# A two-layer encoder: both mixers written as one stream of half weight blocks with attention rounds between them

## The chip, the cores and the metric

One Trainium2 chip (trn2), one core of it. The time is the device time of one execution in microseconds (us); the figure for a kernel is the median of several runs. Engines are called PE (TensorE; PEld its weight loads), DVE (VectorE), ACT (ScalarE), POOL (GpSimd) and SP (SyncE, here a DMA queue).

## What is computed

Input x is 256 tokens of 1024 float32 channels. Two layers follow, each a token mixer and a channel mixer, each closed by x <- LayerNorm(alpha * x + sublayer(x)).

```python
def hybrid_mixer(x, w_in, w_out, beta_mix, ...):
    proj = x @ w_in                      # 1024 -> 3072: q, k, v of 16 heads of 64
    ...
    oa = diff_attention(...)             # A: 4 heads, two softmax maps each, p0 - lam * p1, RMS norm
    ob = dilated_attention(...)          # B: 6 heads, three dilated windows merged
    oc = neighbourhood_attention(...)    # C: 6 heads, 2-D windows with a position bias
    merged = concatenate([oa, ob, oc])
    return (merged * beta_mix) @ w_out   # 1024 -> 1024
```

The channel mixer of layer 0 is a dense SwiGLU (width 2816), that of layer 1 a SwiGLU with 8 experts of width 3584, two per token. Partial rotary is applied to q and k of A and B.

## The kernel before

All matrix products of weights are made in split form: a value is the sum of a rounded part (`_hi`) and the remainder (`_lo`), and each product takes three matmuls (hi*hi, lo*hi, hi*lo; `with_hi` L1358, `three` L1363). Weights come in units of 1 MB (`UNIT`): SP loads a unit into one of six `raw` buffers (`load` L434), ACT makes `w_hi` (`split_hi` L596), DVE `w_lo` (`split_lo` L857), in three buffers each. So each unit costs ACT and DVE one instruction, and PE 24 matmuls of 512 columns. `w_in` has 12 units (u = 0 to 11: six blocks of 512 columns, each in two halves of the input channels), `w_out` four (two rows of 128 each). The tokens are two tiles (tt = 0, 1). Here a *half block* is one unit for one token tile: 12 matmuls.

Nothing schedules at run time: each engine has its program, written out in order, and waits on semaphores. What stands behind a waiting instruction waits too.

Attention is cut into 20 groups (`GROUPS`, L397): 0 to 3 and 4 to 7 are the A heads for the first and second token tile (one head, two maps), 8 to 10 and 11 to 13 are B (two heads), 14 to 16 and 17 to 19 C (two heads). A round of a group a is, in order: `scores` (L1523, PE, 6 matmuls of 256 columns), `row_max` (L914, DVE; for B and C an addition of a bias first), `exps` (L623, ACT), for A also `mix_maps` (L935, DVE), `prob_transposes` (L1542, PE), `prob_copy` (L638, ACT), `weigh_values` (L1556, PE), and after the last group of a segment `merge` (L947, DVE). `qk_group` (PE L1509, ACT L615, DVE L875) transposes q and k of proj in eight groups of four 128x128 tiles and splits them.

Order before, in each layer (PE L1574 on, ACT L691 on, DVE L1060 on): the input is transposed (`operand`, L1377), then `column_units` (L1391) runs each unit for both token tiles. q/k groups 0 and 1 come after unit 3, scores 0 and 1 after unit 4, and from unit 5 on (`SLOTS`, L415) one A round stands behind each unit. After unit 11 all other q/k groups are made, then rounds 8 to 19 run with nothing between them; three splits for the output projection stand among them (`SPLIT_AFTER`, L417). Then the merged heads are transposed into `xT` (`operand`), and `row_units` (L1424) makes the output projection: units 0 and 1 for each token tile, then 2 and 3. `norm_and_operand` (L1012) follows on DVE.

POOL prepares the position bias of C: `padded_rows` (L520) reads the bias rows with one DMA and writes them to a scratch in HBM; `toeplitz` (L537) reads them back shifted, 2304 pieces of 256 bytes for each of two DMAs, and adds the mask with a tensor_tensor on POOL (L549). In layer 0 SP issues no load from unit 3 on until the scratch is written:

```python
if l == 0 and u == NH:
    sp.wait_ge(scratch_in, 32)
load(BASE_IN[l] + u, columns(w_in[l], u // 2, u % 2, 2, CW))
```

## Time and profile before

| | |
|---|---|
| median of 3 runs | 1332.92 us (1327.78 to 1335.93) |
| profiled execution, its own time | 1329.73 us |
| its span, first to last instruction | 1327.7 us |
| mean granted TensorE clock, of full | 0.945 |
| PE / DVE / ACT / POOL busy | 1250.4 / 904.4 / 707.4 / 58.3 us |
| DMA moved | 300.13 MB, mean 226 GB/s |

Busy time is the sum of an engine's instructions; DMA issues, waits and branches don't count. A row of the order in time gives start, duration, engine, source line, operation, tiles, shapes, how many like it in a row (x8), and in brackets how long the engine had been idle and what ended that. A duration can overlap the next start a little; spacing of starts is the surer measure. The clock is the one granted to TensorE, 1.00 for 2.4 GHz and 0.50 for 1.2 GHz.

### The profile page before, as it was taken

The page shows a single profiled execution, that of the slowest core. Times are in us where ns is not written, and L with a number is a line of the kernel's source. Part 1 is how long each engine was busy: PE and PEld are TensorE (multiplying, and loading weights), DVE is VectorE, ACT ScalarE, POOL GpSimd, SP SyncE. Part 2 cuts the span into 40 slices and gives each one's busy share as a digit, 9 for nine tenths or more (in the row PEclk, how much of TensorE's full clock was granted, in tenths as well). Part 3 has the DMA queues.
Part 4 walks back from the last instruction along what each step waited for, and adds up shares of the span by engine and source line. Part 5 has one row for each costly group of instructions (what it writes and reads, how often), then busy time and mean ns, then how long its engine had stood idle before and what let it go on. Part 6 is the DMA issues. An engine that isn't in the chain of part 4 may idle for free.

```text
span 1327.7 us, 14942 instructions
## 1 busy us (share of the span) xinstructions
PE 1250.4 (94%) x5856; PEld 1028.4 (77%) x5856; DVE 904.4 (68%) x840; ACT 707.4 (53%) x721; POOL 58.3 (4%) x47
## 2 busy tenths in 40 slices
PE   7897999999998999499999999999999999999994
PEld 6676878887876788488888888878888888777883
DVE  3657465444466664568888767878877798886673
ACT  4445344433344452166776655766765576775550
POOL 2200020000042000000000000000000000000000
PEclk9896799999998958599999999999999999999997
DMA  9921165554565000198889888898888889888750
GB/s 294 321 96 64 42 211 192 164 210 165 190 179 193 1 1 0 69 356 305 306 296 317 287 320 280 302 331 312 291 291 317 309 288 323 298 309 289 299 192 35
DMA packets 126788, 300.13 MB, mean 226 GB/s; under 512 B 4938, under 2 KB 7128, under 8 KB 126704
## 3 DMA queue, kind: packets, MB, share of 16 engines
q1 hardware_dynamic: 124304, 291.52, 63.3%
q0 software_dynamic: 2112, 6.87, 1.8%
q8 instruction: 51, 0.84, 0.3%
q10 hardware_dynamic: 288, 0.63, 0.1%
q14 instruction: 33, 0.27, 0.1%
HBM read 297.88 MB, written 1.12 MB: 225 GB/s over the span
## 4 chain that ended last, share of the span: by engine, by line
PE 82%; DVE 6%; issue 4%; ACT 3%; DMA 2%; POOL 2%; DVEq 0%; POOLq 0%; SPq 0%; ACTq 0%
PE bank L1360 19%; PE bank L1361 19%; PE bank L1418 13%; PE bank L1705 12%; PE bank L1446 6%; PE bank L1718 6%; ACT w_hi L601 2%; DMA raw<-in_w_in 1%; PE bank L1669 1%; DVE soft L932 1%; PE bank L1566 1%; PE bank L1685 1%; DVE w_lo L860 1%; DVE neg_max L933 1%; POOL w_lo L558 1%
## 5 line engine op out<-in xcount | busy, mean ns | idle before, releaser
L860 DVE TENSOR_TENSOR w_lo<-raw,w_hi 128x2048 fp32r<-128x2048 f32 x273 | 620.9, 2290 | 319.1 <-ACT w_hi L601 317.7
L601 ACT ACTIVATE w_hi<-raw 128x2048 fp32r<-128x2048 f32 x275 | 523.9, 1917 | 322.8 <-PE bank L1418 161.6
L1360 PE MATMUL bank<-w_hi,xT_hi 128*128 128x512 f32 (+1 forms) x896 | 353.0, 395 | 8.0 <-DVE xT_lo L872 3.2
L1361 PE MATMUL bank<-w_hi,xT_lo 128*128 128x512 f32 (+1 forms) x896 | 348.5, 390 | 0.0
L1418 PE MATMUL bank<-w_lo,xT_hi 128*128 128x512 f32 (+1 forms) x832 | 219.7, 387 | 0.0
L1360 PEld LDWEIGHTS bank<-w_hi,xT_hi 128*128 128x128 f32 x896 | 171.0, 191 | 44.1 <-ACT xT_hi L612 6.1
L1361 PEld LDWEIGHTS bank<-w_hi,xT_lo 128*128 128x128 f32 x896 | 171.0, 191 | 34.2
L1418 PEld LDWEIGHTS bank<-w_lo,xT_hi 128*128 128x128 f32 x832 | 154.6, 189 | 33.0 <-DVE w_lo L860 1.0
L1360 PE MATMUL bank<-w_hi,hT_hi 128*128 128x512 f32 x312 | 123.7, 397 | 1.8 <-issue 1.8
L1361 PE MATMUL bank<-w_hi,hT_lo 128*128 128x512 f32 x312 | 123.0, 394 | 0.0
L1705 PE MATMUL bank<-w_hi,xs 128*128 128x512 f32 x336 | 94.3, 402 | 0.0
L1705 PE MATMUL bank<-w_lo,xs 128*128 128x512 f32 x336 | 91.9, 395 | 0.0
L1446 PE MATMUL bank<-w_lo,hT_hi 128*128 128x512 f32 x312 | 85.1, 394 | 0.0
L1705 PEld LDWEIGHTS bank<-w_lo,xs 128*128 128x128 f32 x336 | 63.3, 188 | 14.7
L1705 PEld LDWEIGHTS bank<-w_hi,xs 128*128 128x128 f32 x336 | 61.3, 189 | 13.2
L1360 PEld LDWEIGHTS bank<-w_hi,hT_hi 128*128 128x128 f32 x312 | 58.8, 188 | 16.0 <-issue 2.4
L1446 PEld LDWEIGHTS bank<-w_lo,hT_hi 128*128 128x128 f32 x312 | 58.8, 188 | 13.8
L1361 PEld LDWEIGHTS bank<-w_hi,hT_lo 128*128 128x128 f32 x312 | 58.8, 188 | 13.4
L562 POOL TENSOR_TENSOR rstd<-var_eps,tab 128x1 f32<-128x1 f32 x8 | 12.2, 1521 | 1090.5 <-DVE var_eps L997 1090.4
L1566 PE MATMUL bank<-proj,soft 128*128 128x64 f32 x256 | 50.7, 362 | 0.0
L1566 PEld LDWEIGHTS bank<-proj,soft 128*128 128x128 f32 x256 | 50.6, 289 | 0.0
L1718 PE MATMUL bank<-w_hi,hs 128*128 128x512 f32 x168 | 47.2, 402 | 0.0
(208 smaller groups left out, 1004.5 us busy)
## 6 DMA issues: line engine op xcount, KB each, us to landing
raw<-in_moe_w_gate SPq DMA_DIRECT2D x70, 1024.0 KB, 5.4
raw<-in_moe_w_up SPq DMA_DIRECT2D x70, 1024.0 KB, 5.5
raw<-in_moe_w_down SPq DMA_DIRECT2D x70, 1024.0 KB, 5.4
raw<-in_w_in SPq DMA_DIRECT2D x24, 1024.0 KB, 8.5
raw<-in_ffn_w_gate SPq DMA_DIRECT2D x11, 1024.0 KB, 5.1
raw<-in_ffn_w_up SPq DMA_DIRECT2D x11, 1024.0 KB, 5.2
raw<-in_ffn_w_down SPq DMA_DIRECT2D x11, 1024.0 KB, 5.0
raw<-in_w_out SPq DMA_DIRECT2D x8, 1024.0 KB, 5.0
```

Of the source, the lines that this page charges most:

```text
L558: nc.gpsimd.tensor_tensor(w_lo[:, split % NH, :], raw[:, split % NR, :], w_hi[:, split % NH, :].bitcast(F32), ALU.subtract).then_inc(lo_do ...
L601: nc.scalar.activation(w_hi[:, n % NH, :], raw[:, n % NR, :], ACT.Copy).then_inc(hi_done, 1)
L860: nc.vector.tensor_tensor(w_lo[:, n % NH, :], raw[:, n % NR, :], w_hi[:, n % NH, :].bitcast(F32), ALU.subtract).then_inc(lo_done, 1)
L932: link(nc.vector.scalar_tensor_tensor(sc, s2, HD ** -0.5, bias, ALU.mult, ALU.add))
L933: nc.vector.tensor_reduce(nm, sc, AX.X, ALU.max, negate=True).then_inc(max_done, 1)
L1360: nc.tensor.matmul(o, hi, wh, start=start, stop=False)
L1361: nc.tensor.matmul(o, lo, wh, start=False, stop=False)
L1418: ins = nc.tensor.matmul(o, xh[:, kt, t], wl[:, k, :], start=False, stop=kt == KT - 1)
L1446: ins = nc.tensor.matmul(bank[:, b0 + 2 * tt + ch, :], xh[:, 2 * i + k, t], wl[:, 2 * k + ch, :], start=False, stop=i == last and k == 1)
L1566: ins = nc.tensor.matmul(bank[:, O_BANK[seg], col:col + HD], probT[:, ga % 2, i * NT + kt, :], proj[:, kt, v0 + h * HD:v0 + (h + 1) * HD], ...
L1705: ins = nc.tensor.matmul(bank[:, b, :], xs[:, kt, :], wv[:, k, :], start=kt == 0 and ready is None, stop=kt == KT - 1 and ready is not None)
L1718: ins = nc.tensor.matmul(bank[:, b0 + ch, :], hs[:, 2 * i + k, :], wv[:, 2 * k + ch, :], start=i == 0 and k == 0 and ready is None, stop=i ...
```

## The change

What it does, in each layer:

- PE goes through the 12 units of `w_in` by half blocks (`column_half`), unit by unit, token tile by token tile. Behind a half block (u, tt) stands what the tables say: `QK_AT` q/k groups, `SLOT_AT` one attention round, `MERGED_AT` transposes of merged heads. 14 of the 20 rounds (A and B) stand in the projection.
- Rounds 14 to 19 (C) stand between the eight half blocks of the output projection, in an order written out (`out_half`). The merged heads are transposed and split in five groups (`merged_group`) into `qk_hi`, `qk_lo`, which are twice as large.
- A round's scores use one PSUM bank instead of two, with the values of an earlier group between the two halves and a wait of PE for its own first half (`score_half`).
- `proj_copy` copies each token tile of proj when it is done. In ACT's and DVE's programs the order follows PE's; splits of the output projection's units 0, 1 and 2 stand in the projection.
- The first rotary moves from after unit 2 to before the split of unit 3 on DVE, the second from u = 6 to (5, 1).
- POOL reads the bias rows in reverse by seven DMAs; the shifted copy goes straight into `bias_c`, and the mask is added by DVE (`masked_bias`) behind (9, 1) instead of by POOL. POOL issues its later DMAs without that wait.
- A's `merge` is cut in `squares` and `merge_a`, one slot apart.

The arithmetic is the same. The diff, cut to its core (of the removed lines only some; they stand in the listing above):

```diff
-            qk_hi = sb("qk_hi", [P, KT, SEQ], F32R, scope=s)
-            qk_lo = sb("qk_lo", [P, KT, SEQ], F32R, scope=s)
+            qk_hi = sb("qk_hi", [P, 2 * KT, SEQ], F32R, scope=s)
+            qk_lo = sb("qk_lo", [P, 2 * KT, SEQ], F32R, scope=s)
             bias_c = sb("bias_c", [P, HC, 6, GRID_W], scope=s)
             soft = sb("soft", [P, 12 * SEQ], scope=s)
...
+        SLOT_AT = {(4, 1): 0, (5, 0): 1, (5, 1): 2, (6, 0): 3, (6, 1): 4, (7, 0): 5, (7, 1): 6, (8, 0): 7, (8, 1): 8,
+                   (9, 0): 9, (9, 1): 10, (10, 0): 11, (11, 0): 12, (11, 1): 13}
+        IN_SLOTS = len(SLOT_AT)
+        FIRST_AT = ((3, 1), (4, 0))
+        QK_AT = {(2, 1): (0, 1), (6, 0): (2, 3), (7, 0): (4,), (10, 0): (5, 6)}
+        QK_BANK = [2, 3, 4, 5, 4, 4, 5, 6]
+        MERGED_AT = {(11, 0): (0, 1)}
+        MERGED_BANK = [4, 5, 7, 0, 1]
+        N_MERGED = len(MERGED_BANK)
+        SCORES_IN = IN_SLOTS + 2
...
-                pool.dma_start(rpb_rows[:], na_rpb[l].rearrange("h r c -> r h c")[
-                    NA_ROWS - ROWS:NA_ROWS + ROWS - 1]).then_inc(pad_in, 16)
+                for r in range(7):
+                    pool.dma_start(rpb_rows[r:r + 1], na_rpb[l].rearrange("h r c -> r h c")[
+                        NA_ROWS + ROWS - 2 - r:NA_ROWS + ROWS - 1 - r]).then_inc(pad_in, 16)
                 nc.gpsimd.memset(bias_c[0:7], 0.0).then_inc(pad_zero, 1)
-                pool.wait_ge(pad_in, 16 * (l + 1))
+                pool.wait_ge(pad_in, 7 * 16 * (l + 1))
...
-                    pool.dma_start(shifted[rl * GRID_W:(rl + 1) * GRID_W], src).then_inc(toeplitz_in, 16)
-                pool.wait_ge(toeplitz_in, 32 * (l + 1))
-                pool.wait_ge(consts_in, 16)
-                mask = const("mask_c").unsqueeze(1).broadcast_to([P, HC * 6, GRID_W])
-                nc.gpsimd.tensor_tensor(bias_c[:].rearrange("p h j c -> p (h j) c"), shifted[:, :, ::-1], mask,
-                                        ALU.add).then_inc(bias_ready, 1)
+                    dst = bias_c[rl * GRID_W:(rl + 1) * GRID_W].rearrange("p h j c -> p (h j) c")
+                    pool.dma_start(dst, src).then_inc(toeplitz_in, 16)
...
+                    for tt in range(NT):
+                        if (u, tt) == (3, 0):
+                            act.wait_ge(lam_summed, l + 1)
+                            nc.scalar.activation(lam_exp[:], lam_sum[:], ACT.Exp).then_inc(lam_exped, 1)
+                        if u % 2:
+                            proj_copy(l, u, tt)
+                        for k in QK_AT.get((u, tt), ()):
                             qk_group(l, k)
-                    if u < U_IN - NH:
...
+                        for m in MERGED_AT.get((u, tt), ()):
+                            merged_group(l, m)
+                        if (u, tt) in FIRST_AT:
+                            exps(l, FIRST_AT.index((u, tt)))
+                        if (u, tt) in SLOT_AT:
+                            a = SLOT_AT[u, tt]
+                            prob_copy(l, a)
+                            if a + 2 < SCORES_IN:
+                                exps(l, a + 2)
+                        if (u, tt) == (1, 1):
+                            static_split(BASE_IN[l] + NH)
+                        if u > 0 and tt == 1:
+                            static_split(BASE_IN[l] + u + NH)
+                qk_group(l, 7)
+                prob_copy(l, 14)
+                exps(l, 16)
+                prob_copy(l, 15)
+                merged_group(l, 2)
+                exps(l, 17)
+                prob_copy(l, 16)
+                static_split(BASE_OUT[l] + NH)
+                exps(l, 18)
+                prob_copy(l, 17)
+                exps(l, 19)
+                merged_group(l, 3)
+                prob_copy(l, 18)
+                static_split(BASE_OUT[l] + 1 + NH)
+                prob_copy(l, 19)
+                merged_group(l, 4)
+                static_split(BASE_OUT[l] + 2 + NH)
+                next_operand(2 * l + 1, BASE_OUT[l] + U_OUT - 1)
                 if l == 0:
...
+            def masked_bias(l):
+
+                dve.wait_ge(toeplitz_in, 32 * (l + 1))
+                v = bias_c[:].rearrange("p h j c -> p (h j) c")
+                mask = const("mask_c")[:, ::-1].unsqueeze(1).broadcast_to([P, HC * 6, GRID_W])
+                nc.vector.tensor_tensor(v, v, mask, ALU.add).then_inc(bias_ready, 1)
...
+                    for tt in range(NT):
+                        if (u, tt) == (1, 1):
+                            if l == 0:
+                                dve.wait_ge(consts_in, 16)
+                            rotary(QA, DIFF, DIFF // 8, 2 * WA // DIFF, "a", rope_a[0], rope_a[1], (l * IN_CHUNKS + 1) * NT)
+                            static_split(BASE_IN[l] + NH)
+                        if (u, tt) == (5, 1):
+                            rotary(QB, HD, HD // 8, 2 * HB, "b", rope_b[:, :, 0], rope_b[:, :, 1], (l * IN_CHUNKS + 3) * NT)
+                        for k in QK_AT.get((u, tt), ()):
                             qk_group(l, k)
...
+                        for m in MERGED_AT.get((u, tt), ()):
+                            merged_group(l, m)
+                        if (u, tt) == (3, 0):
+                            lambda_value(l)
+                        if (u, tt) in FIRST_AT:
+                            a = FIRST_AT.index((u, tt))
+                            row_max(l, a)
+                            mix_maps(l, a)
+                        if (u, tt) in SLOT_AT:
+                            a = SLOT_AT[u, tt]
+                            if a in SEG_END[0:2]:
+                                squares(l, SEG_END.index(a))
+                            if a == SEG_END[2]:
+                                merge(l, 2)
+                            if a + 2 < SCORES_IN:
+                                row_max(l, a + 2)
+                            if a + 2 < SEG_END[1]:
+                                mix_maps(l, a + 2)
+                            if a - 1 in SEG_END[0:2]:
+                                merge_a(l, SEG_END.index(a - 1))
+                        if u > 0 and tt == 1:
+                            static_split(BASE_IN[l] + u + NH)
+                        if (u, tt) == (2, 1):
+                            dve.wait_ge(small_in, 48 + 16 * l)
+                            if l == 0:
+                                split_router()
+                            lambda_terms(l)
+                        if (u, tt) == (9, 1):
+                            masked_bias(l)
+                qk_group(l, 7)
+                merge(l, 3)
+                row_max(l, 16)
+                merged_group(l, 2)
+                row_max(l, 17)
+                static_split(BASE_OUT[l] + NH)
+                row_max(l, 18)
+                merge(l, 4)
+                row_max(l, 19)
+                merged_group(l, 3)
+                static_split(BASE_OUT[l] + 1 + NH)
+                merge(l, 5)
+                merged_group(l, 4)
+                norm_and_operand(2 * l, 4, BASE_OUT[l] + U_OUT - 1, 2 * l + 1)
...
+                    q, k = (q0 + h // 2, slice(qt * P, (qt + 1) * P)), k0 + h // 2
+                    if i:
+                        if between:
+                            between()
+                        pe.wait_ge(score_half, ga + 1)
+                    ins = three(bank[:, ga % 2, i * SEQ:(i + 1) * SEQ], qk_hi[part, q[0], q[1]], qk_lo[part, q[0], q[1]],
+                                qk_hi[part, k, :], qk_lo[part, k, :], True, True)
+                    ins.then_inc(score_psum if i else score_half, 1)
...
+                tile_ready, next_tile, after = operand(
+                    2 * l, token_tile,
+                    lambda tt: pe.wait_ge(ln_done, 2 * NT * l + tt + 1 - NT) if l else pe.wait_ge(x_in[tt], 16), 1 if l else 0)
+                for tt in range(NT):
+                    for part in range(2):
...
+                            if j == 4:
+                                pe.wait_ge(qk_lo_in, 8 * l + 5)
+                        column_half(BASE_IN[l] + u, u % 2, tt, proj_banks(j))
+                        for k in QK_AT.get((u, tt), ()):
...
+                        for m in MERGED_AT.get((u, tt), ()):
+                            merged_group(l, m)
+                        if (u, tt) in FIRST_AT:
+                            qk_ready(l, 2)
+                            scores(l, FIRST_AT.index((u, tt)))
+                        if (u, tt) in SLOT_AT:
+                            a = SLOT_AT[u, tt]
+                            if a + 2 in (SEG_END[1], SEG_END[1] + 2, SEG_END[3]):
+                                qk_ready(l, {SEG_END[1]: 4, SEG_END[1] + 2: 5, SEG_END[3]: 7}[a + 2])
+                            if a - 1 in (0, SEG_END[1]):
+                                pe.wait_ge(proj_in, (l * IN_CHUNKS + {0: 2, SEG_END[1]: 4}[a - 1]) * NT)
+                            scores(l, a + 2, (lambda: weigh_values(l, a - 1)) if a else None)
+                            prob_transposes(l, a)
+
+                pe.wait_ge(m_lo, N_MERGED * l + 2)
+                out_half(l, 0, 0)
+                qk_group(l, 7)
+                weigh_values(l, 13)
+                prob_transposes(l, 14)
+                out_half(l, 1, 0)
...
+                scores(l, 16, lambda: weigh_values(l, 14))
+                prob_transposes(l, 15)
+                merged_group(l, 2)
+                pe.wait_ge(m_lo, N_MERGED * l + 3)
+                out_half(l, 0, 1)
+                scores(l, 17, lambda: weigh_values(l, 15))
+                prob_transposes(l, 16)
+                out_half(l, 1, 1)
+                scores(l, 18, lambda: weigh_values(l, 16))
+                prob_transposes(l, 17)
+                scores(l, 19, lambda: weigh_values(l, 17))
+                merged_group(l, 3)
+                prob_transposes(l, 18)
+                pe.wait_ge(m_lo, N_MERGED * l + 4)
+                out_half(l, 2, 0)
+                weigh_values(l, 18)
+                prob_transposes(l, 19)
+                out_half(l, 3, 0)
+                weigh_values(l, 19)
+                merged_group(l, 4)
+                pe.wait_ge(m_lo, N_MERGED * l + 5)
+                out_half(l, 2, 1)
+                out_half(l, 3, 1)
+                making = operand(2 * l + 1, token_tile, lambda tt: pe.wait_ge(ln_done, 2 * NT * l + tt + 1), 1)
```

## Rows read from the trace of the kernel before

**Rows 1.** The page, part 1: busy time and share of the span.

```profile
PE 1250.4 (94%) x5856; PEld 1028.4 (77%) x5856; DVE 904.4 (68%) x840; ACT 707.4 (53%) x721; POOL 58.3 (4%) x47
```

**Rows 2.** Stretches: start:end, their length, then busy time of each engine, clock, DMA.

```profile
394.60:455.20 60.60, 54.71 (x275) 43.37 (x274) 39.29 (x65) 25.79 (x55) 8.42 (x5) 0.94 0.37 119
455.20:509.00 53.80, 48.85 (x268) 44.44 (x267) 34.41 (x53) 30.30 (x75) 1.12 (x1) 0.59 0.00 1
```

**Rows 3.** PE in order of time, layer 1: start, duration, operation, idle before it.

```profile
384.26 1.07 PE L1418 MATMUL bank<-w_lo,xT_hi 128*128 128x512 f32 x4
...
386.98 1.07 PE L1418 MATMUL bank<-w_lo,xT_hi 128*128 128x512 f32 x4
...
411.75 0.59 PE L1365 MATMUL bank<-qk_hi 32*128 32x256 f32 x2 [5.24 <-ACT soft L632]
...
530.14 1.07 PE L1446 MATMUL bank<-w_lo,xT_hi 128*128 128x512 f32 x4
```

**Rows 4.** PE in order of time, layer 0.

```profile
38.46 1.97 PE L1516 MATMUL bank<-tab,proj 128*128 128x128 f32 x8 [3.88 <-DVE proj L892]
40.08 0.77 PE L1360 MATMUL bank<-w_hi,xT_hi 128*128 128x512 f32 x1
...
44.88 0.40 PE L1360 MATMUL bank<-w_hi,xT_hi 128*128 128x512 f32 x1
...
109.83 0.40 PE L1365 MATMUL bank<-xT_hi,qk_hi 64*128 64x256 f32 x2
...
110.89 1.00 PE L1566 MATMUL bank<-proj,soft 128*128 128x64 f32 x8
...
171.53 0.84 PE L1446 MATMUL bank<-w_lo,xT_hi 128*128 128x512 f32 x3
```

**Rows 5.** VectorE in order of time, layer 1: A groups, then B groups with a split.

```profile
409.75 0.69 DVE L921 TENSOR_REDUCE neg_max<-bank 128x2 f32<-128x512 f32 x1
...
443.88 0.17 DVE L943 RECIPROCAL rsum<-sums 128x2 f32<-128x2 f32 x1 [0.83 <-ACT soft L632]
...
444.93 0.42 DVE L961 COPY oa<-bank 128x256 f32<-128x256 f32 x1
...
469.16 0.68 DVE L932 SCALAR_TENSOR_TENSOR soft<-bank,tab 128x512 f32<-128x512 f32 x1
...
473.52 2.29 DVE L860 TENSOR_TENSOR w_lo<-raw,w_hi 128x2048 fp32r<-128x2048 f32 x1 [2.96 <-ACT w_hi L601]
...
478.37 0.18 DVE L956 RECIPROCAL rsum<-sums 128x6 f32<-128x6 f32 x1
...
479.65 0.68 DVE L932 SCALAR_TENSOR_TENSOR soft<-bank,bias_c 128x512 f32<-128x512 f32 x1
```

**Rows 6.** ScalarE in order of time, layer 1: exponentials and a w_hi split.

```profile
410.68 0.47 ACT L632 ACTIVATE soft<-bank,neg_max 128x256 f32<-128x256 f32 x1 [3.62 <-DVE neg_max L922]
...
411.59 1.08 ACT L703 ACTIVATE proj<-bank 128x512 f32<-128x512 f32 x2
...
470.60 0.51 ACT L632 ACTIVATE soft<-soft,neg_max 128x256 f32<-128x256 f32 x1 [2.25 <-DVE neg_max L933]
...
471.60 1.89 ACT L601 ACTIVATE w_hi<-raw 128x2048 fp32r<-128x2048 f32 x1
```

**Rows 7.** VectorE in order of time, layer 1, the product of the lambdas.

```profile
399.63 5.13 DVE L903 TENSOR_TENSOR lam_prod<-lam_in 128x64 f32<-128x64 f32 x1
```

**Rows 8.** GpSimd in order of time: bias rows (layer 0) and mask addition (layer 1).

```profile
1.39 0.76 POOL L524 DMA_DIRECT2D rpb_rows<-in_na_rpb  x1 [0.57 <-issue]
...
399.00 5.67 POOL L549 TENSOR_TENSOR bias_c<-soft,tab 128x2304 f32<-128x2304 f32 x1 [7.28 <-DMA soft<-rpb_scratch]
```

**Rows 9.** Waits of the queue on SP, 0 to 60 us.

```profile
SPq L439 <- DMA rpb_scratch<-bias_c: 10.6, 1, 10.6
```

**Rows 10.** ScalarE in order of time, layer 0, splits of units 4 and 5.

```profile
30.23 1.92 ACT L601 ACTIVATE w_hi<-raw 128x2048 fp32r<-128x2048 f32 x1 [2.61 <-DMA raw<-in_w_in]
32.90 1.92 ACT L601 ACTIVATE w_hi<-raw 128x2048 fp32r<-128x2048 f32 x1 [0.75 <-DMA raw<-in_w_in]
```

369 lines of the change are left out of this document (170 added, 199 removed).

## Prediction, made before the changed kernel ran

> **What bounds the kernel now.** I start with the page's first part: PE (TensorE) is busy for 94% of the span [rows 1], so time can only come from PE's waits, from its slow stretches, or from work that it need not do. I then ask for stretches around the two mixers [rows 2]. In layer 1 the projection runs from 394.6 to 455.2 at a mean clock of 0.94, and the rest of the attention, alone on PE, from 455.2 to 509.0 at 0.59, nearly always "busy" (48.85 of 53.80 us). Layer 0 has such a stretch too, between 96 and 149. At the full clock one round of group B or C costs PE 2.06 us (109.83 to 111.89, [rows 4]), so 12 rounds are 25 us of work: some 28 us a layer look like room. The third view, VectorE and ScalarE in order of time, says why that room is smaller: in the attention stretch VectorE and ScalarE wait for each other in turn [rows 5, 6]. After the row maximum at 469.16 come the exponentials (470.60), then the w_hi split (471.60), then w_lo (473.52). The four follow one another, because each engine works in its written order. The change moves this same chain beside the projection; it doesn't shorten it.
>
> **The change, part by part (layer 1).** PE's work stays the same: one half block is 2.72 us (386.98 less 384.26, [rows 3]), unit 2 ends at 387.9. Now transposes of q/k group 0 and 1 follow (1.0 us, half of row 38.46's time [rows 4], as they run at the full clock), unit 3 (5.44) and the first score half (0.5 with its wait): the first row maximum starts at 395.0. From there I add up what VectorE has to pass in its written order until the split of unit 14 (the third of the output projection) is done:
> - A group, eight times: maximum to exponential 0.93 (409.75 to 410.68), exponential 0.91 (410.68 to 411.59), hand-over 0.14, mix 1.05 (443.88 to 444.93): 3.03 each, 24.2 [rows 5, 6].
> - four splits behind such a group: w_hi starts when the exponential is done and takes 1.95, so VectorE waits 0.77 after the mix, and w_lo takes 2.2: 2.98 each, 11.9.
> - B or C maximum, eight times 1.32 (an estimate: two operations of 0.69 and 0.69 that overlap a little, as row 469.16 starts it): 10.6.
> - five splits behind such a group. From 469.16 to 473.52 are 4.36, of which 1.32 is the maximum: a wait of 3.04, then 2.2: 5.25 each, 26.2. For the last, one more exponential and one copy stand ahead: 0.7.
> - rotary B 1.7, five q/k remainders of 0.62, twice squares and the merge of A (1.45 + 1.28), one merge of B 1.28 (478.37 to 479.65), two merged remainders 1.1: together 12.7 (1.7 + 3.1 + 5.5 + 1.3 + 1.1). The small ones are estimates from rows of like size [rows 5].
> - the mask, new on VectorE: 2304 columns where 2048 take 2.29 [rows 5]: 2.5.
>
> The sum is 88.8 us: 395.0 to 483.8. PE needs over the same eight units 43.5 plus eight A rounds (about 1.3, half the transposes and values of a B round) plus five or six B rounds of 2.06 plus 27 transposes, some 69 us. **So the stream is no longer bound by PE but by the VectorE/ScalarE chain, by about 19 us.** On PE this will show as waits at the second half of scores or at the values, at the q/k transposes of 6,0 (for the rotary), and at the merged groups of 11,0.
>
> From 483.8 I follow the written tail in the same way. The remainder of q/k group 7: 484.5. Scores 16 with values 14: 486.6. Maximum 16, exponential, copy 15, both parts of merged group 2: 490.7, for which PE waits. Half block (0,1): 493.5; round 17/15/16: 495.5; half (1,1): 498.2. ScalarE and VectorE meanwhile: maximum 17 at 495.1, exponential to 497.6, copy 16, w_hi(15), w_lo(15): 502.2; maximum 18, exponential 18, copy 17: 505.2. PE has nothing between some 500 and 505.2, since values 17 need that copy. Scores 19: 506.4; maximum 19, exponential, merged group 3: 510.1; half (2,0), values 18, transposes 19, half (3,0), values 19: 517.8; merge 5 and merged group 4 (1.3 + 0.4 + 0.6 + 0.6): 520.8; two half blocks: 526.3. Before, the last matmul group starts at 530.14 and ends at 531.05 [rows 3]. At the full clock layer 1 gains 4.7 us.
>
> **The clock.** Before, after 3.88 us without a matmul behind unit 3, the eight transposes at 38.46 take 1.97 and the next half block runs from 40.08 to 44.88: 4.8 against 2.72, 2.1 us more [rows 4]. The new tail has three stretches that are thin in this way: 482.9 to 490.7, 498.2 to 510.1, 517 to 520.8. I charge 5 us a layer (two and a half times 2.1), with 0 and 10 as ends: 0 if small matmuls hold the clock, 10 if the thin rounds in them and in the stream run slowly too. Layer 1 then stands at +0.3.
>
> A rule bears on this: in the Trainium skill, page "TensorE: Matmul & The Clock Gate", section "What's actually happening", the clock is halved by default and TensorE's busy-ness releases it. Were busy time enough, the 53.8 us stretch of rows 2, 91% busy, would not stand at 0.59; the row disagrees, so busy time alone is no shelter. By the rule I would charge about 1 us a layer less for the tail, and the sum would be 2 us lower.
>
> **What goes for certain.** In layer 1 PE waits 5.24 us at 411.75 [rows 3]. The reason is VectorE's product of the lambdas, 5.13 us at 399.63 for 64 columns [rows 7], just while GpSimd's mask addition runs (399.00, 5.67 us [rows 8]). That addition leaves GpSimd. The gain is inside the sum above (my 395.0 has none of it). In the Trainium skill, page "SBUF — State Buffer", section "Who interferes with whom", a VectorE instruction with two SBUF inputs is blocked by a GpSimd instruction that reads SBUF; by it the 5 us are gone, and were it the wait for the lambda table's DMA instead, they would stay and layer 1 would be 5 us later.
>
> **Layer 0** starts later. SP holds the loads from unit 3 on until the scratch rows are written, 10.6 us of wait [rows 9]; units 4 and 5 are still waited for at 30.23 and 32.90 [rows 10]. One DMA issue of the bias rows becomes seven on GpSimd's queue: six more at 0.5 to 0.8 each are 3.0 to 4.8 (0.76 is the row of the present one [rows 8]), less what the memset behind them hides; I take 3.3 and shift both splits. w_hi(4) ends at 35.3, the q/k copies at 36.4, w_hi(5) at 38.4; VectorE does w_lo(4), two remainders, w_lo(5) by 41.1 and the router and lambda pieces by 42.7, where the first maximum starts. Adding 526.3 - 395.0 = 131.3 gives 174.0, with the clock 179.0, against 172.4 before (171.53 + 0.84, [rows 4]): +6.6. The 3.88 us wait for the rotary before unit 4 does go, but what is late next is the split of unit 5. Ends: 0 of delay (3.3 less) and 5 (1.7 more).
>
> The layer norms behind both mixers keep their place: the norm of the first 128 tokens again starts some 5.7 us before the last matmul. The wait that scores now make between their halves costs 0.1 to 0.2 each, 40 times, 4 to 8 us if PE were the bound; since it isn't, I take 0. Splits and loads of the output projection are earlier than needed.
>
> **Sum.** +0.3 + 6.6 = +6.9 us. The profiled execution took 1329.73 us (span 1327.7 and 2.0 around it), 3.2 below the median of the runs shown, 1332.92. Added to the median: 1340.
>
> **Rivals.**
> 1. The chain overlaps better than I add it, and PE bounds the stream. For it: before, at seven rounds over eight units, VectorE kept up. Against: twice the rounds now, and the steady 10.5 us for three rounds and a split before (469.16 to 479.65, [rows 5]) is what my terms give (three maxima, 3.04, 2.2, a merge). All of it would bring 19 us a layer less 1 to 2 us of waits, some 35 us, 1305; half of it 1322 or less. I take 1310.
> 2. The lower clock enters the stream, and the kernel is slower: half blocks of 2.72 us stand between rounds of 1.3 to 2.1 us and waits, where before 5.44 us stood for each round. It decides once the clock falls in the B part (seven half blocks, six rounds): 7 x 2.1 + 6 x 1.6 = 24 us on PE, of which about 9 lie in waits that exist anyway: 15 a layer at most, 1370; for half the time 1355. For it: the clock of 0.59 under rounds alone. Against: full-width matmuls are still more than half of the time, and the rounds at 109.83 ran at the full level.
> 3. The change does nothing net: my own case with the clock's charge at 0, -3 us, 1330. It lies inside the forecast's range.
>
> **How the numbers follow.** My own case (with rival 3) has 0.70, its own range 1326 to 1352: the clock's ends give 5 us to either side per layer, the load's ends 3. Rival 1 has 0.17, rival 2 0.13. A measurement of this kernel tells about 1% (13 us) from no change. Rival 1 is faster by more than that. Of my case 0.53 stays within 1% (1319.6 to 1346.3) and 0.17 lies above; with rival 2 slower is 0.30. The range for 8 times in 10 reaches into both rivals: 1318 to 1360.
>
> **What would show it.** In the changed profile: (a) no wait like that at 411.75 and no 5 us product of the lambdas; (b) the first row maximum of layer 1 at about 395, of layer 0 at about 42.7; (c) VectorE in w_lo(14) about 89 us after the first maximum, with waits for w_hi of 3 us each behind B and C groups; (d) PE idle between matmuls in the second half of the stream, released by ScalarE's copies of the probabilities and by VectorE; (e) in the tail PE waits of 3 to 5 us before (0,1), values 17 and (2,1), with the clock below 1 there; (f) last output matmul near 531 less what layer 0 adds, i.e. 134 to 138 us after the first maximum. I am wrong if w_lo(14) ends under 80 us after the first maximum (rival 1), or if half blocks in the middle of the stream take over 4 us (rival 2).

## The result and the profile after

The changed kernel takes 1340.75 us (median of 13 runs, 1336.44 to 1346.82) against 1327.78 for the kernel before, measured beside it (13 runs, 1324.94 to 1335.93). The ratio is 1.0086, with a 95% interval of 1.0065 to 1.0106: slower by 0.9%, inside the forecast's range and its "within 1%". The profiled execution has a span of 1341.5 us, 13.8 more than before. The sum of the prediction said +6.9, the medians beside each other say +13.0. The forecast of 1340 met 1340.75 by luck: it was added to 1332.92, the median of three runs of the kernel before, which is 5.1 us above the median of the 13 runs measured beside the changed kernel. My own case with its range held the result, its working did not, as the experiments show.

The page of the changed kernel: busy time, then PE and its clock in 40 slices.

```profile
PE 1261.3 (94%) x5856; PEld 1022.9 (76%) x5856; DVE 904.1 (67%) x844; ACT 706.5 (53%) x723; POOL 54.7 (4%) x57
...
PEclk9999689999999998679999999999999999999997
```

PE has 10.9 us more of busy time than before [rows 1], for the same matmuls (5856 in number). The low digits of the clock are slices 5 and 6 (from 134 us, layer 0's tail) and 16 to 18 (from 503 us, layer 1's tail and the router behind it).

Stretches of the changed kernel: layer 1's steady part of group B, layer 1 from the first row maximum to the end of the projection, then for layer 0 and layer 1 the stretch from the last half block of the projection to the end of the output projection ("the tail" from here on). Columns: start:end, length, busy time (and count) of PE, PEld, DVE, ACT and POOL, clock, DMA share, GB/s.

```profile
455.00:470.00 15.00, 15.00 (x85) 12.05 (x84) 10.56 (x17) 8.62 (x23) 1.01 (x1) 1.00 0.00 1
...
406.67:485.10 78.43, 77.72 (x404) 60.85 (x404) 53.69 (x88) 40.84 (x91) 2.98 (x4) 1.00 0.30 102
...
120.35:184.10 63.75, 52.38 (x233) 41.76 (x234) 28.25 (x40) 19.46 (x41) 2.16 (x2) 0.76 0.20 66
485.10:545.90 60.80, 49.00 (x234) 39.36 (x234) 26.02 (x39) 15.77 (x39) 1.52 (x1) 0.83 0.00 1
```

The first row contradicts the prediction's main step: PE does not wait at all where I had put the chain of VectorE and ScalarE 19 us above it. Before, the attention stretch ran at a clock of 0.59 [rows 2]; the stream runs at 1.00.

VectorE and GpSimd of the changed kernel in order of time (start, duration, operation, idle before it).

```profile
404.61 0.22 DVE L967 TENSOR_TENSOR lam_prod<-lam_in 128x64 f32<-128x64 f32 x1
...
406.67 0.69 DVE L985 TENSOR_REDUCE neg_max<-bank 128x2 f32<-128x512 f32 x1 [0.91 <-PE bank L1451]
...
462.64 2.29 DVE L914 TENSOR_TENSOR w_lo<-raw,w_hi 128x2048 fp32r<-128x2048 f32 x1 [2.97 <-ACT w_hi L643]
...
474.00 2.55 DVE L944 TENSOR_TENSOR bias_c<-bias_c,tab 128x2304 f32<-128x2304 f32 x1
...
492.91 2.29 DVE L914 TENSOR_TENSOR w_lo<-raw,w_hi 128x2048 fp32r<-128x2048 f32 x1 [3.60 <-ACT w_hi L643]
...
9.68 2.29 DVE L914 TENSOR_TENSOR w_lo<-raw,w_hi 128x2048 fp32r<-128x2048 f32 x1 [1.25 <-ACT w_hi L643]
...
9.95 2.22 POOL L577 COPY bias_c<-rpb_rows 7x186 f32<-7x186 f32 x1 [2.86 <-DMA rpb_rows<-in_na_rpb]
12.47 1.23 POOL L580 DMA_DIRECT2D rpb_scratch<-bias_c  x2 [0.30 <-POOL bias_c L577]
```

The product of the lambdas takes 0.22 us, where it took 5.13 [rows 7]; the wait of 5.24 at 411.75 [rows 3] is gone. The first row maximum of layer 1 is at 406.67; as layer 1 starts 10.96 us later, that is 395.7 in the frame of before (395.0 predicted), and 41.93 in layer 0 (42.7 predicted). w_lo(14) ends at 495.1 in layer 1, 88.4 us after the first maximum (88.8 predicted), and VectorE's waits for w_hi of 2.97 are there. All of this looked like a hit. But 88.4 is also what PE needs to that point: its half block (1,0) of the output projection ends at 495.1 too, and from the first maximum to the end of the projection (406.67 to 485.10) PE is busy for 77.7 of 78.4 us, with a longest wait of 0.5.

PE in layer 1's tail, changed kernel: the matmuls with a wait of over 1 us before them.

```profile
502.34 0.80 PE L1444 MATMUL bank<-w_hi,qk_hi 128*128 128x512 f32 x1 [2.80 <-DVE qk_lo L936]
...
519.12 1.97 PE L1712 MATMUL bank<-proj,soft 128*128 128x64 f32 x8 [3.54 <-ACT soft L698]
...
525.62 0.80 PE L1444 MATMUL bank<-w_hi,qk_hi 128*128 128x512 f32 x1 [1.91 <-DVE qk_lo L936]
...
536.75 0.55 PE L1661 MATMUL bank<-tab,proj 128*128 128x128 f32 x3 [1.47 <-DVE proj L1054]
538.47 0.50 PE L1444 MATMUL bank<-w_hi,qk_hi 128*128 128x512 f32 x1 [1.17 <-DVE qk_lo L936]
```

The output projection ends at 545.9, 139.2 us after the first maximum (136.3 predicted with the clock); in layer 0 at 184.1, which is 142.2 after it. Against the kernel before [rows 3, 4] layer 0 loses 11.7 us (6.6 predicted) and layer 1 another 3.7 (0.3 predicted).

### The profile page after: what moved, and what is told of

Same layout as the page of the kernel before. It is cut to its first block, busy times and chain, and to the rows that moved or that the text cites. A ratio compares the mean times of both kernels' runs of the same rounds, so it can differ in the third digit from the quotient of the medians.

```text
span 1341.5 us, 14964 instructions
## 1 busy us (share of the span) xinstructions
PE 1261.3 (94%) x5856; PEld 1022.9 (76%) x5856; DVE 904.1 (67%) x844; ACT 706.5 (53%) x723; POOL 54.7 (4%) x57
## 4 chain that ended last, share of the span: by engine, by line
PE 77%; DVE 10%; ACT 5%; issue 4%; DMA 2%; POOL 1%; DVEq 0%; POOLq 0%; ACTq 0%; SPq 0%
PE bank L1444 18%; PE bank L1445 18%; PE bank L1861 12%; PE bank L1502 10%; PE bank L1874 6%; PE bank L1530 5%; ACT w_hi L643 3%; DVE w_lo L914 2%; ACT soft L686 2%; PE bank L1825 1%; DMA raw<-in_w_in 1%; DVE neg_max L999 1%; DVE soft L998 1%; PE bank L1712 1%; PE bank L1630 1%
## 5 line engine op out<-in xcount | busy, mean ns | idle before, releaser
L1444 PE MATMUL bank<-w_hi,xT_hi 128*128 128x512 f32 (+1 forms) x832 | 326.7, 394 | 8.5 <-DVE xT_lo L926 3.2
L1445 PE MATMUL bank<-w_hi,xT_lo 128*128 128x512 f32 (+1 forms) x832 | 321.9, 388 | 0.0
L1444 PEld LDWEIGHTS bank<-w_hi,xT_hi 128*128 128x128 f32 x832 | 157.5, 189 | 42.1 <-ACT xT_hi L654 6.1
L1445 PEld LDWEIGHTS bank<-w_hi,xT_lo 128*128 128x128 f32 x832 | 157.6, 189 | 31.0
L1502 PE MATMUL bank<-w_lo,xT_hi 128*128 128x512 f32 (+1 forms) x640 | 167.9, 385 | 0.0
L1502 PEld LDWEIGHTS bank<-w_lo,xT_hi 128*128 128x128 f32 x640 | 117.9, 188 | 25.0 <-DVE w_lo L914 1.0
L686 ACT ACTIVATE soft<-soft,neg_max 128x256 f32<-128x256 f32 x48 | 24.0, 501 | 88.6 <-DVE neg_max L999 88.6
L1530 PEld LDWEIGHTS bank<-w_lo,hT_hi 128*128 128x128 f32 x312 | 58.8, 188 | 13.8
L1608 PE MATMUL bank<-w_lo,xT_hi 128*128 128x512 f32 x192 | 51.9, 392 | 0.2 <-DVE w_lo L914 0.2
```

Source lines behind the costliest of these rows:

```text
L686: ins = nc.scalar.activation(prob[:, ga % 2, i, :], src, ACT.Exp, bias=neg_max[:, ga % 4, i:i + 1], scale=DIFF ** -0.5 if kind == "a" else ...
L1444: nc.tensor.matmul(o, hi, wh, start=start, stop=False)
L1445: nc.tensor.matmul(o, lo, wh, start=False, stop=False)
L1502: ins = nc.tensor.matmul(o, xh[:, kt, t], wl[:, k, :], start=False, stop=kt == KT - 1)
L1530: ins = nc.tensor.matmul(bank[:, b0 + 2 * tt + ch, :], xh[:, 2 * i + k, t], wl[:, 2 * k + ch, :], start=False, stop=i == last and k == 1)
L1608: ins = nc.tensor.matmul(o, xT_hi[:, kt, t], wl[:, k, :], start=False, stop=kt == KT - 1)
```

## The experiments

All of them are made from the changed kernel unless said otherwise, and compared with its 1340.75. "Stream" is the time from the first row maximum to the end of the last half block of the projection: 78.4 us in both layers of the changed kernel. The tail of the changed kernel is 63.8 us in layer 0 and 60.7 in layer 1. One profile of each kernel is not enough for small differences there: in the five profiles whose tail is written as in the changed kernel (the changed kernel, experiment 1, both of experiment 3, experiment 6) it takes 58.3 to 63.8 us, at a clock of 0.76 to 0.88.

**1. Which engine bounds the stream.** ScalarE's order in slots that hold a split:

```diff
+                            if tt == 1:
+                                static_split(BASE_IN[l] + u + NH)
                             prob_copy(l, a)
                             if a + 2 < SCORES_IN:
                                 exps(l, a + 2)
...
-                        if u > 0 and tt == 1:
+                        if u > 0 and tt == 1 and (u, tt) not in SLOT_AT:
                             static_split(BASE_IN[l] + u + NH)
```

> The changed kernel, with ScalarE's order altered in the seven slots that hold a weight split: w_hi comes ahead of the copy of the probabilities and of the exponentials, so that VectorE need not wait for it (2.97 us each behind B groups, 0.67 behind A groups in the changed kernel's trace). Theory of the prediction (the VectorE/ScalarE chain bounds the stream, 88.8 us): five waits of 3 and some of 0.7 fall away, the stream from the first row maximum to the end of w_lo(14) shortens from 88.4 to some 74 us per layer, the whole by 20 to 28 us, to about 1316. Rival (PE bounds the stream, since the changed trace shows it busy for 15.00 of 15.00 us from 455 to 470 and the waits of VectorE are slack): the stream stays at 87 to 89 us and the whole within 3 us of 1341.

Measured: 1336.71 us; stream 77.0 and 77.6. VectorE did get ahead (w_lo(14) ends 82.8 us after the first maximum in layer 0, 5.6 sooner), and PE gained 0.8 to 1.4 us of it. The chain did not bound the stream; PE did. The total is 4.0 us lower, 1 more than my rival allowed; in the profile the rest of the gain lies in the tail (58.6 and 59.7), which is as it was written before.

**2. The split inside the tail.**

```diff
-                static_split(BASE_OUT[l] + NH)
                 exps(l, 18)
                 prob_copy(l, 17)
                 exps(l, 19)
                 merged_group(l, 3)
+                static_split(BASE_OUT[l] + NH)
```

The same was done on VectorE.

> The changed kernel, with the split of unit 15 (the fourth of the output projection) moved on ScalarE and VectorE from between rounds 17 and 18 to behind the copy of merged group 3. In the changed trace w_hi(15) waits 6.2 us for the half block (0,1) and holds exponential 18 and the copy of the probabilities 17 behind it; PE waits 3.54 us for that copy in layer 1. Theory (the split at that place is what is late): the wait before values 17 goes to about 0 to 1 us, 2.5 to 3.5 us a layer, and with the clock that falls in it up to 5: total 1331 to 1336. Rival (what follows on ScalarE and VectorE is as long anyway, and the next wait takes its place at the half block (2,0)): within 1.5 us of 1341.

Measured: 1333.93 us, in the range expected. The tail is 60.2 and 57.6, 3.6 and 3.2 less; these lengths alone would not show it, the total and the wait do. The wait for values 17 fell from 3.54 to 1.98, and in layer 1 these matmuls ran at the full clock (1.10 in place of 1.97 us; still 1.97 in layer 0). The wait did not go to 0 to 1: in layer 1 ScalarE's copy, which stands behind exponential 18, ends it at 514.4, and merge 4, which frees the bank of the outputs, ends only 0.3 us sooner.

**3. The start of layer 0.** SyncE's hold taken away:

```diff
-                    if l == 0 and u == NH:
-                        sp.wait_ge(scratch_in, 32)
```

> The changed kernel without SyncE's wait for the scratch rows (12.7 us into the span, 10.6 before the change) ahead of the load of weight unit 3. Theory of the prediction (the hold delays units 3 to 5 and with them the first row maximum of layer 0, 41.9): w_hi(3) needs no wait of 4.09 us, units 4 and 5 no wait of 2.36 us, the first row maximum comes 4 to 6 us earlier and the whole is 4 to 6 us shorter, about 1336. Rival (the loads are bound by the bytes moved, the hold only reorders them; the bias rows then wait behind 1 MB loads, with no effect since the masked bias is first needed at 110 us): first row maximum within 1 us of 41.9, total within 1.5 us of 1341.

And one transfer of the bias rows in place of seven. It leaves out the reversal of the rows, so the bias of C is built in the other order and the result is another; the amount of work is the same:

```diff
-                for r in range(7):
-                    pool.dma_start(rpb_rows[r:r + 1], na_rpb[l].rearrange("h r c -> r h c")[
-                        NA_ROWS + ROWS - 2 - r:NA_ROWS + ROWS - 1 - r]).then_inc(pad_in, 16)
+                pool.dma_start(rpb_rows[:], na_rpb[l].rearrange("h r c -> r h c")[
+                    NA_ROWS - ROWS:NA_ROWS + ROWS - 1]).then_inc(pad_in, 16)
```

> The changed kernel with the bias rows of each layer loaded by one transfer again instead of seven, so that they arrive in the order of memory (the bias of the third head group is then built from rows in the other order; the amount of work is the same). Theory of the prediction (six more issues delay the scratch rows and with them the held loads by 3.3 us): the scratch rows leave GpSimd's queue at about 9.2 to 10 instead of 12.47 us, SyncE's hold ends 2 to 3.5 us earlier, the first row maximum of layer 0 stands at 38 to 40 instead of 41.9, total 1337 to 1339. Rival (the loads are bound by their bytes): first row maximum at 41 to 42, total within 1.5 us of 1341.

Measured: without the hold 1334.88 us, first row maximum 37.7, a gain at the upper end of what was expected. With one transfer 1339.52 us, first maximum 39.2: the maximum is where the theory had it, the total is within 1.5 us of the changed kernel, as the rival had it. Its copy of the bias rows starts at 7.37 and takes 0.33 us. In the changed trace the copy took 2.22 us; it had started at 9.95, behind VectorE's w_lo at 9.68. In the kernel of experiment 7 (tail alone), which has the same start, VectorE and GpSimd stand the other way round:

```profile
10.08 2.37 DVE L914 TENSOR_TENSOR w_lo<-raw,w_hi 128x2048 fp32r<-128x2048 f32 x1 [1.24 <-ACT w_hi L643]
...
9.97 0.33 POOL L577 COPY bias_c<-rpb_rows 7x186 f32<-7x186 f32 x1 [2.88 <-DMA rpb_rows<-in_na_rpb]
10.59 1.23 POOL L580 DMA_DIRECT2D rpb_scratch<-bias_c  x2 [0.30 <-POOL bias_c L577]
```

Over all profiled executions with seven transfers and the hold, a copy of 1.62 to 2.48 us goes with a first maximum at 41.7 to 42.8 (five: the changed kernel, experiments 1, 2 and 4, and the first of 5), a copy of 0.33 us with 37.1 to 37.6 (three: the second of 5, experiment 6, and the tail alone of 7). Without the hold the first maximum is at 37.7, 36.3 and 36.4, whatever the copy took (0.33, 2.27, 2.19). So the issues as such cost nothing that shows: with seven and an undisturbed copy the maximum is earlier than with one. What they do is to move the copy from 7.75 to some 9.9 us, where w_lo also starts, between 0.9 us before it and 0.1 after it in these eight. The one that comes second waits.

How some 2 us of the copy become some 5 us of the first maximum is not shown. The hold itself hardly differs: SyncE waits 12.4 to 12.7 us with the late copy and 12.0 to 12.4 with the early one. What differs is the traffic behind it, 90 to 185 GB/s from 18 to 20 us with the late copy and 364 to 380 with the early one, and unit 4, whose split starts at 32.6 to 33.7 against 27.4 to 27.6. That it needs the hold is shown by the three kernels without it.

**4. Is the tail's loss the clock or the waits?** Matmuls that keep nothing, in front of the waits:

```diff
                 merged_group(l, 2)
+                filler(l, 6, 16)
                 pe.wait_ge(m_lo, N_MERGED * l + 3)
                 out_half(l, 0, 1)
...
+                filler(l, 2, 6)
                 pe.wait_ge(m_lo, N_MERGED * l + 5)
```

> The changed kernel with matmuls that compute nothing that is kept: 16 of 128x512 into a free bank ahead of the wait before half block (0,1), and 6 ahead of the wait before (2,1), in both layers. They lie in waits that the changed trace has (2.80 and 1.17 us in layer 1, some more in layer 0) and take about 0.23 us each at the full clock: 3.7 and 1.4 us. Theory (the tail lost some 8 us in layer 1 and 11 in layer 0 to the lower clock, and PE's thin stretches make it fall): half block (0,1) runs in 2.8 instead of about 3.4 us, the stretch from the end of w_lo(14) to the end of the output projection (50.6 and 53.5 us) shortens by 2 to 5 us a layer, total 1332 to 1337. Rival (the clock falls for another reason, or the fillers themselves run slowly and push the half blocks back): the stretch stays or grows by 1 to 3 us a layer, total 1341 to 1347.

Measured: 1339.52 us, against 1340.75 inside the scatter of the runs.

```profile
120.20:180.50 60.30, 52.46 (x256) 42.72 (x256) 28.34 (x40) 19.50 (x41) 2.18 (x2) 0.86 0.22 70
481.35:541.90 60.55, 52.73 (x255) 42.91 (x256) 25.98 (x39) 15.75 (x39) 1.52 (x1) 0.86 0.00 1
```

The tail's clock is 0.86 in both layers, against 0.76 and 0.83, and the tail is 60.3 and 60.6 long: 3.5 less in layer 0, the same in layer 1. All of this lies within what the unchanged tail shows from profile to profile. What the fillers did shows beside them, in layer 1. The half block (0,1) behind the first 16 ran at the full level, 2.89 us (498.91 to 501.80) against 4.41 (502.34 to 506.75); but the fillers took 3.91 us where the wait had been 2.80, and gave some 1 us of that back. The six of the second wait ran at the lower level (2.61 us together, where the wait had been 1.17). Filling the gaps is worth little: the waits remain.

**5. What PE's work in a round consists of.** The two heads' scores in two banks again for rounds 0 to 15, the projection on banks 4 and 5 from its third chunk on, and the transposes of q/k groups 2 to 7 and merged groups 0 and 1 moved; scores 5 and 7 stand behind the values and transposes of their slot. The core:

```diff
+        def score_parts(a):
+            if a < SCORES_IN:
+                return [bank[:, 6 * (a % 2) + i, 0:SEQ] for i in range(2)]
+            return [bank[:, a % 2, i * SEQ:(i + 1) * SEQ] for i in range(2)]
...
-                    if i:
+                    if i and a >= SCORES_IN:
                         if between:
                             between()
-                        pe.wait_ge(score_half, ga + 1)
+                        pe.wait_ge(score_half, l * (NG - SCORES_IN) + a - SCORES_IN + 1)
```

> The changed kernel with the two heads (or maps) of rounds 0 to 15 written to two PSUM banks again (0 and 1, or 6 and 7), without the wait between their matmuls, as before the change; the projection keeps to banks 4 and 5 from its third chunk on, and the transposes of q/k groups 2 to 7 and of merged groups 0 and 1 move to banks and places that are free then. ScalarE's order is as in the changed kernel. Theory (PE bounds the changed stream, and the halves in turn cost it what the traces show: an A round takes 2.1 us against 1.2 before, a B or C round 2.6 against 2.0): from the first row maximum to the end of the last projection half 78.4 falls by up to 8 x 0.9 + 6 x 0.6 = 11 us a layer, but VectorE's chain (9.0 us per two A slots against 9.6 on PE now, 9.3 per two B slots against 10.95) then binds: 6 us a layer, total about 1329. Rival (the halves in turn cost nothing, as the prediction had it, since the chain binds or the 0.1 to 0.2 each are all): within 2 us of 1341.

The same with the order of experiment 1:

> The last kernel (two banks for the scores of rounds 0 to 15) with w_hi ahead of the copy of the probabilities and the exponentials on ScalarE, as in the first experiment. That order alone moved the end of the last projection half by 1 us (77.0 and 77.6 against 78.4). Theory (PE and the chain are nearly level at 78 to 88 us, and shortening one shows only when the other is shortened too): the stream loses 9 us a layer against the changed kernel, to about 69, 3 more than two banks alone; total 1319 to 1324. Rival (the chain has no part in it): the same as two banks alone. Second rival (PE's waits at the moved transposes eat it): above 1330.

Measured: 1363.41 and 1342.73 us; streams 89.9 and 89.5, then 80.3 and 79.9. Both numbers were missed. PE in layer 1, first and second kernel, and VectorE in the second:

```profile
442.22 0.59 PE L1461 MATMUL bank<-qk_hi 32*128 32x256 f32 x2 [5.52 <-issue]
...
457.69 0.39 PE L1461 MATMUL bank<-qk_hi 32*128 32x256 f32 x2 [4.24 <-issue]
```

```profile
425.54 0.39 PE L1463 MATMUL bank<-qk_hi 32*128 32x256 f32 x2 [4.76 <-issue]
...
439.32 0.46 PE L1463 MATMUL bank<-qk_hi 32*128 32x256 f32 x2 [3.49 <-issue]
...
421.96 2.29 DVE L927 TENSOR_TENSOR w_lo<-raw,w_hi 128x2048 fp32r<-128x2048 f32 x1
424.16 1.28 DVE L944 TENSOR_TENSOR qk_lo<-bank,qk_hi 128x512 fp32r<-128x512 f32 x2
```

The profile names no releaser here ("issue"). By the program the scores of rounds 5 and 7 wait for the remainders of the q/k groups that stand in their banks; the second of them ends at 425.44, 0.1 us before the scores start, and on VectorE a w_lo of 2.29 us is written ahead of each remainder. That waits of that size would follow was only my second rival there: they are 4.76 and 3.49 us; the cause is a queue on VectorE that I had not read. Less these 8.25 the second kernel's stream is 71.7, so PE's own work did fall, and the second rival took it. The pair also shows the chain: as soon as PE leans on it, ScalarE's order is worth 9.6 us a layer (89.5 against 79.9), where in experiment 1, with PE as the bound, the same edit moved the stream by some 1.

The price of the halves by itself, on the kernel before:

```diff
                 for i, h in enumerate(heads):
...
+                    if i:
+                        ins.then_inc(score_half, 1)
+                        pe.wait_ge(score_half, ga + 1)
```

> The kernel before the change, with one thing of the change added: PE waits after the first head's (or map's) three score matmuls until they are done before it starts the second's, still in another bank. Theory (the two heads' matmuls run at the same time on different rows of the array before, and in turn after the change): 0.6 to 0.9 us more per round on PE, 24 to 36 us of PE's time in 40 rounds; where attention stands alone the chain of VectorE and ScalarE runs through the scores too, so nearly all of it shows: total 1345 to 1360. Rival (the prediction's value, 0.1 to 0.2 each): 4 to 8 us at most, total 1328 to 1336.

Measured: 1350.06 us, 21.4 us slower than the kernel before beside it (1328.69) (ratio 1.0182, 1.0151 to 1.0213). Score matmuls of an A round, first in the kernel before, then in this one:

```profile
420.35 0.39 PE L1365 MATMUL bank<-qk_hi 32*128 32x256 f32 x2
420.57 0.28 PE L1366 MATMUL bank<-qk_lo,qk_hi 32*128 32x256 f32 x2
420.69 0.28 PE L1367 MATMUL bank<-qk_hi,qk_lo 32*128 32x256 f32 x2
```

```profile
426.79 0.38 PE L1366 MATMUL bank<-qk_hi 32*128 32x256 f32 x1
427.01 0.28 PE L1367 MATMUL bank<-qk_lo,qk_hi 32*128 32x256 f32 x1
427.13 0.27 PE L1368 MATMUL bank<-qk_hi,qk_lo 32*128 32x256 f32 x1
427.46 0.38 PE L1366 MATMUL bank<-qk_hi 32*128 32x256 f32 x1
427.68 0.28 PE L1367 MATMUL bank<-qk_lo,qk_hi 32*128 32x256 f32 x1
427.80 0.28 PE L1368 MATMUL bank<-qk_hi,qk_lo 32*128 32x256 f32 x1
```

Before, each row holds two matmuls (x2), one of each map: they start together, and both maps are through in 0.55 us. With the wait the second map starts 0.67 us after the first. That times 40 rounds is 26.8 us; 21.4 of them show.

**6. GpSimd beside VectorE.** The mask's addition given back to GpSimd:

```diff
+                pool.wait_ge(toeplitz_in, 32 * (l + 1))
+                pool.wait_ge(consts_in, 16)
...
+                nc.gpsimd.tensor_tensor(v, v, mask, ALU.add).then_inc(bias_ready, 1)
...
-                        if (u, tt) == (9, 1):
-                            masked_bias(l)
```

> The changed kernel with the addition of the mask given back to GpSimd, right behind the arrival of the Toeplitz rows, as before the change (5.67 us there), and taken from VectorE (2.55 us at 474.00). Theory (GpSimd's addition blocks VectorE's operation with two inputs in SBUF that runs beside it): in layer 1 the product of the lambdas or whatever of VectorE stands beside it takes some 5 us longer and PE waits up to 5 us; against it 2.55 us of VectorE's go in each layer, which PE hardly feels: total 1342 to 1347. Rival (the 5.13 us of the product were the wait for the lambda table's transfer): the product stays at 0.22 us, total 1337 to 1341.

Measured: 1346.63 us. Streams 82.3 and 84.1 against 78.4.

```profile
408.90 5.10 POOL L597 TENSOR_TENSOR bias_c<-bias_c,tab 128x2304 f32<-128x2304 f32 x1 [8.40 <-DMA bias_c<-rpb_scratch]
...
409.28 0.17 DVE L1014 RECIPROCAL rsum<-sums 128x2 f32<-128x2 f32 x1 [1.09 <-ACT soft L691]
409.48 4.68 DVE L1015 TENSOR_SCALAR soft<-soft,rsum,lam_neg 128x256 f32<-128x256 f32 x1
```

This time the addition (5.10 us) met another instruction of VectorE, a scaling of the probabilities that takes 0.41 us elsewhere: it took 4.68 and ended 0.2 us after the addition. In layer 0 it met a tensor_scalar of two columns at 37.86, 4.77 us in place of 0.17. The product of the lambdas stood clear of the addition and took 0.22. So the 5.13 us of before, which ended 0.1 us after GpSimd's addition [rows 7, 8], are read as the same collision and not as a transfer. The Trainium skill (page "SBUF — State Buffer", section "Who interferes with whom") has both: an instruction with two SBUF inputs contends with a GpSimd instruction that reads SBUF, and tensor_scalar is among those that can contend, the one issued first blocking the other. The prediction's case and this run agree with it.

**7. The order of the tail.** On PE:

```diff
                 out_half(l, 1, 0)
+                merged_group(l, 2)
                 qk_ready(l, 8)
                 scores(l, 16, lambda: weigh_values(l, 14))
                 prob_transposes(l, 15)
-                merged_group(l, 2)
+                scores(l, 17)
                 pe.wait_ge(m_lo, N_MERGED * l + 3)
                 out_half(l, 0, 1)
-                scores(l, 17, lambda: weigh_values(l, 15))
                 prob_transposes(l, 16)
+                scores(l, 18, lambda: weigh_values(l, 15))
+                weigh_values(l, 16)
+                prob_transposes(l, 17)
                 out_half(l, 1, 1)
-                scores(l, 18, lambda: weigh_values(l, 16))
-                prob_transposes(l, 17)
                 scores(l, 19, lambda: weigh_values(l, 17))
...
                 prob_transposes(l, 19)
+                weigh_values(l, 19)
                 out_half(l, 3, 0)
-                weigh_values(l, 19)
```

ScalarE and VectorE follow: the copies of merged group 2 ahead of round 16, the split of unit 15 right behind exponential 17. First with the edits of experiments 1 and 3, then alone.

> The changed kernel with edits of order alone: ScalarE's w_hi first in the slots (1336.71 alone), no hold on SyncE's loads (1334.88 alone), and a new order of the tail: merged group 2 and the scores of round 17 ahead of half block (0,1), the split of unit 15 behind the exponentials of 17, scores 18 and the values of 15 and 16 ahead of (1,1), so that (1,1) covers the merge that merged group 3 and values 17 wait for, and values 19 ahead of (3,0), which covers the last merge. Theory (PE's waits in the tail are the sum of what stands in the written order and each can be covered by a half block; 2.80, 3.54, 1.91, 1.47 and 1.17 us in layer 1 of the changed trace, about 9 with what the orders of splits added): the stretch from the last projection half to the end of the output projection falls from 60.7 and 63.8 to 51 to 54 us, the whole to 1314 to 1322, under the kernel before the change (1328). Rival (the tail is bound by the sum of PE's own work at a lower clock, the waits only move): the stretch stays above 57, the whole at 1326 to 1332.

> The changed kernel with the new order of the tail alone (as in the kernel with order alone, but w_hi in the slots and the hold on the loads as in the changed kernel). Theory (the size that the prediction missed, some 9 us a layer behind the last projection half, is waits in a written order, with the lower clock as their consequence): the stretch from the last projection half to the end of the output projection falls from 63.8 and 60.7 to 48 to 51 us, the whole by some 22 us, to 1316 to 1322, under the kernel before. Rival (the three edits of order help only together): above 1326.

Measured: together 1308.72 us (ratio to the kernel before 0.9852, 0.9832 to 0.9872), tail 48.8 and 47.8. Alone 1323.07 us (0.9968, 0.9938 to 0.9997), 1 us above the range expected, tail 53.0 and 54.1, which is 2 and 3 us above the 48 to 51 I expected; its first maximum of 37.3 in layer 0 is part of the gain in the profiled execution. Both pairs of tails lie well below the 58.3 to 63.8 of the old order. Tails of both kernels, together first:

```profile
113.87:162.62 48.75, 44.15 (x232) 35.45 (x231) 24.85 (x34) 19.22 (x37) 2.17 (x2) 0.93 0.22 73
463.10:510.90 47.80, 43.20 (x231) 34.70 (x231) 22.65 (x33) 15.49 (x35) 1.52 (x1) 0.96 0.00 1
```

```profile
115.70:168.70 53.00, 46.40 (x232) 36.82 (x231) 27.62 (x39) 19.74 (x41) 2.14 (x2) 0.90 0.25 80
470.00:524.20 54.20, 47.57 (x232) 37.92 (x231) 25.46 (x38) 16.03 (x39) 1.52 (x1) 0.87 0.00 1
```

**8. Everything.** The kernel "together" of experiment 7 with two banks, where the scores of rounds 5 and 7 come behind the next half block and w_lo(8) and w_lo(9) behind the remainders. PE's part, against the kernels of experiment 5:

```diff
+                            if a in (4, 6):
+                                qk_ready(l, a if a == 4 else 5)
+                                scores(l, a + 1)
                             if a in (3, 5):
                                 weigh_values(l, a - 1)
                                 prob_transposes(l, a)
-                                qk_ready(l, 4 if a == 3 else 5)
-                                scores(l, a + 2)
```

> The last kernel (order alone) and the two PSUM banks for the scores of rounds 0 to 15, now with the scores of rounds 5 and 7 put behind the next half block, and VectorE's w_lo(8) and w_lo(9) behind its remainders of q/k groups 2, 3 and 4: in the earlier kernel with two banks PE waited 4.76 and 3.49 us for these remainders, since a w_lo of 2.29 stood ahead of each. Theory (with these waits gone the stream is PE's own work less the halves in turn): from the first row maximum to the end of the last projection half 79.9 falls to 70 to 73 us a layer, against about 77.5 in the kernel with order alone; total 4 to 7 us a layer lower than that one, 1300 to 1312. Rival (the chain of VectorE and ScalarE, which PE's speed has now caught up with, binds at 76 to 78 us): within 3 us of the kernel with order alone.

Measured: 1291.03 us (ratio 0.9720, 0.9699 to 0.9741), under the expected range: the best kernel of the study, 2.8% below the kernel before and 3.7% below the changed one. Its two streams and tails:

```profile
36.42:105.90 69.48, 66.33 (x396) 52.53 (x395) 55.17 (x90) 41.80 (x95) 2.07 (x2) 1.00 0.56 193
105.90:153.72 47.82, 43.22 (x239) 34.83 (x236) 25.98 (x36) 19.88 (x38) 2.16 (x2) 0.96 0.24 81
376.21:445.68 69.47, 66.64 (x398) 52.91 (x397) 55.16 (x90) 41.36 (x94) 3.28 (x5) 1.00 0.34 117
445.68:493.56 47.88, 43.28 (x239) 34.90 (x236) 23.79 (x35) 16.15 (x36) 1.52 (x1) 0.96 0.00 1
```

The stream is 69.5 us in both layers, 8.0 less than with order alone (77.5), and its waits of over 1 us in layer 1 are down to 1.10 and 1.65 (1.24 and 1.61 in layer 0). ScalarE has w_hi first in both kernels, so the 8.0 us are what the second bank, and the places and order that go with it, bring.

## Why the prediction was right, point by point

The time was right, in part by the luck of the median it was added to; of its steps these held and these failed.

- **"So the stream is no longer bound by PE but by the VectorE/ScalarE chain, by about 19 us": wrong.** The sum of the chain (88.8 against 88.4) was no proof of it, because PE's own work to that point is as long. The term that failed is "some 69 us" for PE: measured are 78.4. The 19 us also compare two different points, PE's work to the last half block of the projection with the chain's to w_lo(14). PE had 10.0 us more to do to that point (485.1 to 495.1), so by my own 69 the lead of the chain was some 10 us. I priced a B or C round at 2.06 and an A round at 1.3, from rounds in which the two heads run at once [rows 4]. In the changed kernel they share a bank and run in turn:

```profile
458.05 0.38 PE L1449 MATMUL bank<-qk_hi 64*128 64x256 f32 x1
458.27 0.28 PE L1450 MATMUL bank<-qk_lo,qk_hi 64*128 64x256 f32 x1
458.39 0.28 PE L1451 MATMUL bank<-qk_hi,qk_lo 64*128 64x256 f32 x1
458.60 1.10 PE L1712 MATMUL bank<-proj,soft 128*128 128x64 f32 x8
459.63 0.38 PE L1449 MATMUL bank<-qk_hi 64*128 64x256 f32 x1
459.86 0.28 PE L1450 MATMUL bank<-qk_lo,qk_hi 64*128 64x256 f32 x1
459.97 0.28 PE L1451 MATMUL bank<-qk_hi,qk_lo 64*128 64x256 f32 x1
460.19 0.55 PE L1699 MATMUL bank<-tab,soft 128*128 128x128 f32 x3
```

The first head, the values, the second head, the transposes: 2.55 us from 458.05 to the next half block at 460.60, against 1.99 before (109.83 to 111.82). In the A part a half block and a round take 4.78 us (417.99 to 422.77), 1.87 of them for the round (to 419.86); before it was 1.20 (420.35 to 421.55). Experiment 8, with the halves undone, has a stream of 69.5.
- **"The wait that scores now make between their halves costs 0.1 to 0.2 each ... since it isn't, I take 0": wrong twice.** The price is 0.55 to 0.7 a round and PE is the bound. It is the change's largest hidden cost: experiment 8 gets 8.0 us a layer back for 16 of 20 rounds, and the kernel before loses 21.4 when only this is added (experiment 5). I weighed the wait and not the concurrency that it ends. The rows above tell the two apart: the values cover the wait (the second head starts right behind them, at 459.63), and still each head takes some 0.55 us, where both together took that before (109.83 to 110.39). Experiment 5's 0.67, with nothing between the halves, has some 0.1 of waiting in it. The diff shows both: the bank of a head was `2 * (ga % 2) + i`, now it is `ga % 2`.
- **The mask (2.5 predicted, 2.55 measured) and "In layer 1 PE waits 5.24 us ... That addition leaves GpSimd": held,** and experiment 6 shows the cause.
- **"I follow the written tail": right in kind, too short.** From the end of w_lo(14) I had 42.5 us and 5 for the clock. Measured are 50.7 and 53.7. Split by the windows: the same matmuls take 43.2 us of PE's time in the tail at a clock of 0.96 (experiment 7, together), 49.0 and 52.4 in the changed kernel. That is some 5.8 us for the clock in layer 1 (5 charged) and 9.2 in layer 0 (up to 10 allowed for), in this execution; other profiles of the same tail have 58.3 to 63.2 us. What is left, 44.9 and 44.5, is some 2 us over the walk in each layer. The waits that I named in front of (0,1), values 17 and (2,1) are all there (2.80, 3.54, and 1.47 and 1.17). A fourth, 1.91 in front of (2,0), I had not named, but the walk has it: 3.7 us from scores 19 to (2,0), measured 3.6 (522.1 to 525.6). What the walk lacked beside the clock is in part the halves again: round 17/15/16 takes 2.54 us (506.75 to 509.29) and not 2.0.
- **"six more at 0.5 to 0.8 each ... I take 3.3": time right, cause wrong.** The copy on GpSimd lost a race with w_lo in this execution; where it won, the first maximum came at 37.1 to 37.6 (experiment 3). The issues delay the copy by 2.2 us, and where it then ran undisturbed that cost nothing. I had neither the race nor that it matters only with the hold, though the rule of the Trainium skill that I used for the lambdas covers the race (page "SBUF — State Buffer", section "Who interferes with whom").
- **Rival 1 (PE bounds the stream, 1310)** named the right engine and the wrong time, since it took PE's work at 69 us too. My sign for it, w_lo(14) under 80 us after the first maximum, could not show it: the split of unit 14 needs the buffer of unit 11, which PE leaves only at 78.4. Even in experiment 1, with the chain ahead, w_lo(14) ends at 82.8. **Rival 2** (the lower clock enters the stream) did not occur: 1.00 throughout.

The sum missed 6.9 us: about 5 in layer 0 and 3.4 in layer 1, nearly all of it in the tail, less some 1.6 elsewhere. That the stream came out at its forecast length was luck as well: the chain's sum and PE's real work happened to meet at the same point. Had the chain been shorter, as experiment 1 makes it, PE's true 78.4 would have stood in the way of the gain that I would have forecast.

## What to carry to other kernels

When a duration is taken from a trace, look at what ran beside it: "x2" in a row of PE meant two heads at once, and a change of their bank undid that. A forecast that two bounds meet needs both sums done with equal care, and an experiment that shortens one bound alone tells which it is; here the shorter chain alone paid some 1 us a layer, and PE's shorter work on top of it 8. And where two stages are woven into one, write out the end of the stream on every engine: the order there was worth about 1% by itself.

## What the runs showed of the hardware that I had not expected

- Matmuls on different rows of the array run at the same time (two maps of three matmuls each in 0.55 us), and with a wait between them the second starts 0.67 us after the first. The Trainium skill, page "TensorEngine Tiling (Array Packing)", section "Gotcha 1: PSUM Pressure", says that different row tiles cannot use the same PSUM bank simultaneously; this kernel's wait keeps to that. No run here tried the same bank without it, so whether the rule holds here is not shown.
- VectorE's operation with scalars (tensor_scalar) is held as long by GpSimd's addition as one with two tensors: 4.68 us for 0.41, and even one of two columns, 4.77 for 0.17.
- Which of two instructions up to 0.9 us apart on VectorE and GpSimd comes first went with some 5 us of the first maximum in layer 0: a copy of 186 columns took 2.22 us behind w_lo and 0.33 ahead of it, and w_lo 2.29 or 2.37. It differs between kernels whose start is written alike, and a single profile shows only one of the two.
- The tail at waits of 11.8 us in 60.8 had a clock of 0.83, at 4.6 in 47.8 one of 0.96; removing waits paid in clock as well, some 5.8 us of 12.9 in layer 1. The same written tail differs by up to 5.5 us between profiles, at clocks of 0.76 to 0.88.
